# All units of the projection in one piece ahead of a step's other products

## What is computed

```python
h = rmsnorm(x, norm_mix_pre)
z = h @ w_in                      # one projection, 4880 columns
aq, ak, av, mq, mk, mv, mo, gate_pre, ga, gm = split(z)
a_out = axial_gqa(aq, ak, av) @ w_attn_o          # softmax attention, 8 heads, 2 kv heads
m_out = bidir_mlstm(mq, mk, mv, mo, gate_pre) @ w_mlstm_o   # 4 heads, two directions
merged = sigmoid(ga) * a_out + sigmoid(gm) * m_out
x = x + rmsnorm(merged @ w_out)
# then a gated feed-forward part with a width-3 convolution
```

## Time and profile before

| | |
|---|---|
| median of 3 runs | 2652.83 us (2650.03 to 2653.18) |
| the profiled execution | 2649.2 us, span 2647.4 us |
| TensorE busy in the span | 2473.7 us (93%) |
| VectorE, ScalarE, GpSimd busy | 1700.6, 886.3, 533.2 us |
| mean granted clock of TensorE | 0.968 of full speed |
| attention stage | about 200 to 736 us of the span |
| mLSTM stage | about 736 to 1181 us |

### The profile page before, as it was taken

One profiled execution on the slowest core, in us unless ns is written; L12 is line 12 of the kernel. 1 busy time (PEld: TensorE's weight loads), 2 busy tenths in 40 slices (PEclk: granted clock), 3 DMA queues, 4 the chain that ended last, 5 costly groups with the idle time before them and its releaser, 6 DMA issues.

```text
span 2647.4 us, 32694 instructions
## 1 busy us (share of the span) xinstructions
PE 2473.7 (93%) x11264; PEld 2025.4 (77%) x11264; DVE 1700.6 (64%) x2301; ACT 886.3 (33%) x1398; POOL 533.2 (20%) x442
## 2 busy tenths in 40 slices
PE   7879999999989999984999999999999999999995
PEld 6767777777768788863887878888888888888883
DVE  5526887877656767655445556576576576576577
ACT  4325644555445555545103321111111111111113
POOL 2522333233235455542220000000000000000004
PEclk9989999999999999996999999999999999999998
DMA  7655342443463635324555311101101101101105
GB/s 221 191 161 136 103 146 81 126 143 94 142 176 104 197 107 168 103 73 162 199 176 154 108 49 40 32 24 40 32 24 40 32 24 40 32 24 40 32 24 190
DMA packets 286617, 263.89 MB, mean 100 GB/s; under 512 B 20520, under 2 KB 227624, under 8 KB 286512
## 3 DMA queue, kind: packets, MB, share of 16 engines
q1 hardware_dynamic: 281184, 249.44, 31.8%
q10 hardware_dynamic: 5328, 13.11, 1.3%
HBM read 193.25 MB, written 69.26 MB: 99 GB/s over the span
## 4 chain that ended last, share of the span: by engine, by line
PE 50%; issue 1%; POOL 1%; DMA 1%; DVE 0%; ACT 0%; POOLq 0%; SPq 0%; ACTq 0%; DVEq 0%
PE pVal L81 7%; PE pVal L79 7%; PE pVal L80 7%; PE pG L79 5%; PE pG L81 5%; PE pG L80 5%; PE pD L80 2%; PE pD L79 2%; PE pD L81 2%; PE pY L79 2%; PE pY L81 2%; PE pY L80 2%; PE pB L79 2%; PE pB L81 2%; PE pB L80 2%
## 5 line engine op out<-in xcount | busy, mean ns | idle before, releaser
L2163 DVE TENSOR_TENSOR y_sum<-y_sum,pVal 128x512 f32<-128x512 f32 x240 | 163.4, 688 | 215.8 <-PE pVal L81 215.8
L1933 POOL TENSOR_TENSOR y_sum<-y_sum,branch_hi 128x1024 f32<-128x1024 f32 x12 | 28.4, 2363 | 1240.3 <-DVE y_sum L2198 1240.3
L79 PE MATMUL pG<-branch_hi,wg_hi 128*128 128x512 f32 x528 | 208.9, 396 | 2.4 <-issue 2.4
L81 PE MATMUL pG<-branch_lo,wg_hi 128*128 128x512 f32 x528 | 208.8, 396 | 0.0
L80 PE MATMUL pG<-branch_hi,wg_lo 128*128 128x512 f32 x528 | 208.8, 395 | 0.0
L81 PE MATMUL pVal<-branch_lo,wv_hi 128*128 128x512 f32 x528 | 205.6, 389 | 0.0
L80 PE MATMUL pVal<-branch_hi,wv_lo 128*128 128x512 f32 x528 | 205.4, 389 | 0.0
L79 PE MATMUL pVal<-branch_hi,wv_hi 128*128 128x512 f32 x528 | 205.4, 389 | 0.0
L566 DVE TENSOR_TENSOR win_lo<-win_raw,win_hi 128x1024 fp32r<-128x1024 f32 x96 | 127.0, 1322 | 106.8 <-ACT win_hi L560 106.5
L1296 POOL TENSOR_TENSOR w_sum<-w_sum,w_all 128x512 f32<-128x512 f32 (+3 forms) x128 | 151.5, 1184 | 195.3 <-DVE w_all L1398 173.9
L1995 ACT ACT_TABLE_LOAD x22 | 28.2, 1283 | 479.8 <-DVE conv L2145 479.8
(11 more groups left out here) (283 smaller groups left out, 6314.5 us busy)
## 6 DMA issues: line engine op xcount, KB each, us to landing
win_raw<-in_w_in SPq DMA_DIRECT2D x96, 512.0 KB, 4.2
zT_scratch<-z_st SPq DMA_DIRECT2D x96, 256.0 KB, 4.4
ffn_raw<-in_w_up SPq DMA_DIRECT2D x44, 512.0 KB, 3.9
sig<-zT_scratch SPq DMA_DIRECT2D x16, 768.0 KB, 6.2
ffn_raw<-in_w_down SPq DMA_DIRECT2D x22, 512.0 KB, 4.4
hT_hi<-hT_hi_scratch SPq DMA_DIRECT2D x40, 256.0 KB, 5.0
hT_lo<-hT_lo_scratch SPq DMA_DIRECT2D x40, 256.0 KB, 5.5
m_raw<-zT_scratch SPq DMA_DIRECT2D x36, 256.0 KB, 3.4
```

Source lines behind the costliest of these rows:

```text
L79: pe.matmul(out, w_hi, x_hi, start=first, stop=False, **kw)
L81: return pe.matmul(out, w_hi, x_lo, start=False, stop=last, **kw)
L1933: pool.tensor_tensor(r, r, x_row(t), ALU.add).then_inc(f_added, 1)
L2163: dve.tensor_tensor(y_sum[:, t, cut(h)], y_sum[:, t, cut(h)], down_bank(2 * t + h), ALU.add).then_inc(s.summed, 1)
```

## The change

In each step of attention the units due were issued in three parts: the first ahead of the turned tops and the weighing, the second (a third of them, rounded down) between weighing and scores, the third between the two halves of the step's pieces. In each item of the mLSTM they were issued in two parts, the second (half of them, rounded down) behind the weighing. Now all of them are issued at the first place. Numbers, waits and the other engines' programs are as before. The units ahead of and behind the loops (`LAST_PART`, and the first ones of the mLSTM) stay where they were.

```diff
--- before.py
+++ after.py
@@ -1089,12 +1089,11 @@
             pe.wait_ge(fixed_v, 2)
             for i in slots():
                 due = DUE[i + LEAD]
-                project(due - 2 * (due // 3))
+                project(due)
                 for u in starting(i + 3):
                     turn_top(u)
                 if i >= 0:
                     weigh(i)
-                project(due // 3)
                 if i + 2 >= 0 and i + 2 < NS:
                     scores(i + 2)
                 for u in ending(i - 1):
@@ -1551,13 +1549,12 @@
                     for j in made_ready(x):
                         prepare(j)
                     due = START + sum(DUE[:x + 1]) - fill.begun
-                    project(due - due // 2)
+                    project(due)
                     n, m = ITEMS[x]
                     t = NS * n + ONE[m][0]
                     if FIRST[t] == x and t + 2 < NS * MH:
                         scores(t + 2)
                     weigh(x)
-                    project(due // 2)
                 for j in after(x, SUMS):
                     denominators(j)
     return used
```

## The result

The changed kernel takes 2664.89 us (median of 6 runs, 2660.47 to 2667.09), the kernel before 2649.32 (6 runs, 2644.29 to 2653.18). The ratio is 1.0056, with a 95% interval of 1.0043 to 1.0068: slower by 11 to 18 us. The forecast was slower by 8.8 us, with a range of its own from 5 to 16; the measured 15.6 lies near its upper end. The predicted 2661 lies close partly by luck, since it was set on a median of 2652.83 that more runs brought down to 2649.3.

What follows compares the result with a forecast made beforehand. TensorE's matmuls were taken to set the time; attention +2.7, mLSTM +4.4 and clock +1.7 summed to +8.8 us on a median of 2652.83, written as 2661. The forecast's own range was 2658 to 2669, the whole 2646 to 2673.

Steps and rivals of the forecast that it cites:

- weighing: Attention: 0.70 us more slack removes 18 of the weighing's 19 waits for `o_sum` and shortens the long one, -7.9 us.
- turned tops: Attention: the turn of the tops comes one unit later after the scores, shortening its one wait of 0.9 us, -0.7 us.
- pieces: Attention steps with four pieces: with two banks and no unit between pairs, piece 3 waits longer for piece 1's reduction, +4.0 us.
- `win_lo`: Attention: the first unit of a group comes earlier and waits for its projection weights in eight groups, +4.5 us.
- `hT_lo`: Attention: units at new token blocks and behind the loop wait longer for activation DMAs issued behind VectorE's `win_lo`, +4.0 us.
- sums and inverse: Attention: these stand at the same distance from the scores as before, so no cost was set.
- switching: Attention: two fewer changes from one product to another per step, at a few ns each, -1.2 us.
- half clock: Both stages: a wait can be followed by a half-clock stretch costing 1.7 us; one stretch more, +1.7 us, from -5 to +14.
- The mLSTM: mLSTM: denominators, one unit nearer behind the weighing, wait longer for `w_sum_lo`; +2.8, +2.1 and -0.5 make +4.4 us.
- Rival (b): Clock: waits vanish and unbroken runs of 12 matmuls save half the clock's 30 us; -8 us, 2645; chance 0.11.
- (a): Both stages: small slacks hold and only waits that exist today move; +3.8 us, 2656.6; chance 0.29.
- (c): Clock: each of the eight longest growing waits brings one half-clock stretch more; +20.7 us, 2673.5; chance 0.10.

Runs made afterwards that it cites:

- e8: Changed kernel, with ScalarE doing its part of the gates ahead of copying the half output: 2663.82 us, ratio 1.0056 to the kernel before.
- e2: Kernel before, with the change made in the mLSTM alone: 2655.49 us, ratio 1.0023.
- e6: Kernel before, with the denominators issued one item later, behind that item's first units: 2642.34 us, ratio 0.9970.
- e1: Kernel before, with the change made in attention alone: 2657.07 us, ratio 1.0030.
- e3: Kernel before, with only attention's unit between weighing and scores moved ahead of the weighing: 2648.91 us, ratio 0.9994.
- e4: Kernel before, with only attention's unit between the halves of the pieces moved ahead of the weighing: 2662.66 us, ratio 1.0050.
- e5: Changed kernel, with one unit kept between the two pairs in attention steps with four pieces: 2664.22 us, ratio 1.0053 to the kernel before.
- e10: Changed kernel with the edits of e6 and e7 (late denominators, early loads): 2632.64 us, ratio 0.9934 to the kernel before.
- e7: Kernel before, with SyncE issuing the activations' loads at the start of its step or item: 2642.34 us, ratio 0.9971.
- e11: Kernel before with the edits of e6 and e7 and the one move of e3: 2628.19 us, ratio 0.9919.

## Why the prediction came out as it did

The side was right, and most terms of the sum were. The order written for one step has a unit too many ("UU W U S p U p U"), but the chain behind it is right, and all distances come from the chain. Attention, by the rows of waits:

| term | forecast | measured |
|---|---|---|
| weighing | -7.9 | -7.3 (15.1 - 3.7 - 17 x 0.24) |
| turned tops | -0.7 | -0.9 (their row is gone) |
| pieces | +4.0 | +3.5 (`att_top` +2.5, `att_tops` +0.6, `q_max` +0.4) |
| `win_lo` | +4.5 | +3.8 (3.2 to 7.0) |
| `hT_lo` | +4.0 | +6.1 (9.9 to 16.0) |
| sums and inverse | 0 | +3.0 (`o_out` 1.1 to 3.1, `att_rwide` 1.3 to 2.3) |
| switching | -1.2 | not to be separated |
| half clock | part of +1.7 | +1.1 (+3.6 by more traces, see below) |

**Weighing, tops, pieces, weights.** "With 0.70 us more slack the 18 vanish (-7.2) and the long one shrinks by 0.7" held: two waits are left. Measuring from the scores gave these four terms to within 0.7 us each. The four-piece step of the earlier trace rows shows its term by itself in the changed kernel; the second pair's wait was 0.52 and is 1.33:

```profile
249.28 0.71 PE L1028 MATMUL pM<-k_stack,q_stack 128*128 128x512 f32 x2
251.32 1.09 PE L1028 MATMUL pM<-k_stack,q_stack 128*128 128x512 f32 x2 [1.33 <-DVE att_top L896]
```

The start-to-start distance is 2.04 us against 1.91 in the earlier trace rows, though a unit's 0.70 is no longer inside it: 0.83 us lost, where I had 0.70.

**Activations.** The three waits that I costed (+1.0, +2.3, +0.7) grew by 1.26 (2.33 to 3.59), 2.05 (2.91 to 4.96) and 0.77 us (3.44 to 4.21): right, and for the reason given, that the issue hangs on SyncE. What failed was to stop there. I asked how late each present wait would be and not whether four units in one piece outrun the landing of their loads: two new waits, 2.5 us, less 0.4 at the small ones.

**"Sums and inverse stand at the same distance from S."** Wrong, +3.0 us. It holds for TensorE and not for ScalarE, where the exponential of those scores queues behind `o_half` and the gate part, which hang on the weighing, and in other steps behind `q_max`, which hangs on the turned tops. In e8 the first part went with ScalarE's order.

**The mLSTM.** +4.4 forecast, +4.6 in the profile, 6 by e2: close by luck, since the make-up was wrong. Of the waits for `w_sum_lo`, 8 were expected in place of 4, each 0.70 longer. Three of the four grew by 0.5 to 0.7 us, one by 0.1, and of the four that were near the threshold only one turned into a wait (0.4 us): +2.4 us, while the scores waited 0.8 us less. The other three kept 0.3 to 1.2 us to spare, more than the 0.05 to 0.3 of before; why isn't shown. What I took for a cost of waits went mostly with the clock: +3.4 us of half clock in the changed kernel, +8.0 in e2.

**Clock.** +1.7 was the term that was most undersized: one stretch more was allowed for. One execution doesn't give its size, for the half clock of a stage varies from one to the next. The traces of the experiments have each stage with the old and with the new order several times:

| us | old order | new order | means |
|---|---|---|---|
| attention | 535.5, 533.6, 532.8 (before, e2, e6) | 544.4, 542.7 (after, e1) | +9.6 |
| of it half clock | 19.4, 15.3, 14.4 | 20.4, 19.5 | +3.6 |
| mLSTM | 435.3, 432.8, 438.0, 435.7 (before, e1, e3, e4) | 439.9, 443.3, 442.8, 440.1 (after, e2, e5, e8) | +6.1 |
| of it half clock | 7.1, 5.4, 10.8, 7.3 | 10.6, 15.1, 12.4, 10.7 | +4.6 |

The two stages come to +15.7 us by these means, which is the whole of the measured 15.6, and up to 8 of them are clock, where I had 1.7. e6 shows the exchange from the other side: 4.8 us of short waits fewer, 8.3 us less of stage.

Rival (b), that unbroken runs of 12 matmuls would earn clock, had nothing for it: in attention the half clock didn't fall. Its reading of the earlier trace rows was also off. The wait just before 826.4 is one of 1.13 us (it ends at 824.72); the one of 1.31 us ended at 785.33, and no stretch follows it. And "what loses the clock are waits of over a us" doesn't hold for all: the stretch at 939.0 in the same trace stands behind a wait of 0.32 us. The rule of the Trainium skill (TensorE: Matmul & The Clock Gate, Part 1, What's actually happening) that activity releases the throttle isn't refuted by that, for TensorE was busy for a smaller share of the stage (510.4 of 535.5 us before, 508.5 of 544.4 after), and e6, with fewer waits and less half clock, agrees with it.

**Behind the mLSTM.** Forecast 1466 us as now; the stage took 2.7 us more, with the same work. No edit reaches it. In all eleven experiments it took 1448.6 to 1451.1 us, with the old order as with the new, against 1447.6 in the trace of before and 1450.3 in that of after: the trace of before is the short one, and I count the 2.7 us as scatter.

**Rivals.** (a), +3.8 us, falls by the interval (11 to 18). (c), +20.7, lies above the interval: it had the right mechanism and too high a price, since not each wait that grew brought a stretch more. The test that mattered came last: e10. It shows that the 15 us aren't the price of the order. They are the price of this order while SyncE issues loads behind stores and the denominators stand right behind the weighing, as I see it; shown is that the two edits together take the difference away, and not how it divides between them. In the profile of e10 attention is cured and the mLSTM only in part.

## What to carry to other kernels

Before a block of work is moved ahead, list for each operand that it needs on what its producer hangs. The producers that hang on the same anchor as before the move cost nothing; a DMA queue that issues loads behind stores, and an engine that serves another product first, do. If such a queue is the cost, reorder the queue and not the matmuls: that was worth some 8 us here (e7), against the 15 that the move lost, and a move whose gain hadn't been visible then gained (e11). And where half-clock stretches are seen behind waits of about 1 us, such a wait is to be counted at more than its length: in e6 4.8 us of waits went with 8.3 us of stage. And a stage's half clock is to be read from several executions before a few us of it are believed.

## What the runs showed of the hardware

**VectorE behind GpSimd.** I had called the long `win_lo` of the earlier trace rows (3.38 us, else 1.22) a meeting with a GpSimd addition worth "2 us either way". The rows are more exact. In the kernel before the addition beside it is

```profile
300.62 2.78 POOL L815 TENSOR_TENSOR p_sum<-p_sum,probs 128x1024 f32<-128x1024 f32 x1 [4.06 <-ACT probs L825]
```

which ends at 303.40, and `win_lo` ends at 304.49, 1.09 us later. In the changed kernel a `p_lo` meets one:

```profile
283.79 2.40 POOL L815 TENSOR_TENSOR p_sum<-p_sum,probs 128x1024 f32<-128x1024 f32 x1 [9.84 <-ACT probs L825]
...
284.83 2.44 DVE L909 TENSOR_TENSOR p_lo<-probs,p_hi 128x1024 fp32r<-128x1024 f32 x1 [0.71 <-ACT p_hi L831]
```

It ends at 287.27, 1.08 us after the addition. So in these meetings a VectorE subtraction of two 128 x 1024 tiles of SBUF that started during such an addition ended about its own length (1.22 us) after it, wherever it began. An `o_sum` that starts inside the same kind of addition (277.80 us before, one operand in PSUM) takes its usual 0.67. The Trainium skill (SBUF — State Buffer, Who interferes with whom) says that a VectorE instruction with two inputs in SBUF contends with a GpSimd instruction that reads SBUF, that this contention is an exclusive lock, and that a VectorE instruction with at most one input in SBUF, outside some faster modes, doesn't contend. The trace agrees: 1.08 and 1.09 us behind the addition for the first kind, the usual 0.67 for the second.

**Short waits and the clock.** Before the change TensorE waited four times for the denominators, 1.31, 1.13, 1.09 and 0.32 us. Behind the last three, 1.7 to 2.7 us after the wait's end, stands a stretch of 3.4 us at a granted clock of 0.50; behind the longest stands none. In the changed kernel the waits were 1.80, 1.82, 1.80, 0.41 and 0.42 us; the first four were followed by such a stretch (6.8, 3.4, 3.4 and 3.4 us), the last wasn't. So short waits in a stage where TensorE is busy 97% of the time can go with half clock, and the length of the wait alone doesn't tell which ones do. What else decides is open.
